# Norm weight and inverse rms split in the FFN of a two-block transformer kernel, and rope totals first in the latent expansion

## The reference, cut to what matters

```python
def _rmsnorm(x, g):
    xf = x.astype(jnp.float32)
    y = xf * lax.rsqrt(jnp.mean(xf * xf, axis=-1, keepdims=True) + EPS)      # EPS = 1e-6
    return (y * g.astype(jnp.float32)).astype(x.dtype)

# first block, its last two steps (D_MODEL = 1024, D_FF = 2816)
x = x + _rmsnorm(_memory_cross_attention(h, mem, ...), norm_mem_post)
h = _rmsnorm(x, norm_ffn_pre)
g, u = jnp.split(h @ w_gate_up, 2, axis=-1)
x = x + _rmsnorm((jax.nn.silu(g) * u) @ w_down, norm_ffn_post)

# second block, latent attention: 4 heads, nope 128 wide, rope 64 wide
q = (_rmsnorm_2(c_q, q_a_norm_w) @ w_uq).reshape(b, s, 4, 192)
kv = (_rmsnorm_2(c_kv, kv_a_norm_w) @ w_ukv).reshape(b, s, 4, 256)
k_nope, v_mla = kv[..., :128], kv[..., 128:]
q_m = _rmsnorm_2(jnp.concatenate([q_nope, q_rope], axis=-1), mla_q_norm_w)
k_m = _rmsnorm_2(jnp.concatenate([k_nope, k_rope], axis=-1), mla_k_norm_w)
o_mla = _mla_attention(q_m, k_m, v_mla)
```

## Time and profile before

| what | value |
|---|---|
| median of 3 runs | 3254.81 us (3250.01 to 3255.03) |
| the profiled execution | 3254.06 us |
| its span, first to last instruction | 3252.3 us |
| mean granted TensorE clock | 0.978 of full |
| TensorE (PE) busy | 3082.2 us, 95% of the span |
| VectorE (DVE) busy | 1711.2 us, 53% |
| GpSimd (POOL) busy | 1373.1 us, 42% |
| ScalarE (ACT) busy | 1053.8 us, 32% |

### The profile page before, as it was taken

How to read it: one execution, slowest core, us unless ns; L and a number is a source line. 1 busy time by engine, 2 the same in 40 slices (tenths; PEclk the granted TensorE clock), 3 DMA queues, 4 the chain that set the end, 5 groups by cost and what they waited for, 6 DMA issues and landing times.

```text
span 3252.3 us, 37435 instructions
## 1 busy us (share of the span) xinstructions
PE 3082.2 (95%) x13379; PEld 2409.0 (74%) x13390; DVE 1711.2 (53%) x2554; ACT 1053.8 (32%) x1638; POOL 1373.1 (42%) x799
## 2 busy tenths in 40 slices
PE   8999998999988899999999799879999989999998
PEld 6788785668776588888888576648766778878886
DVE  3799965545443621121212731135796576666648
ACT  3321215620334300000010333135676366662221
POOL 3254332334432233343434143256000367777878
PEclk9899999999999999999999899999999999999999
DMA  3022410024210011111111113351441247779774
GB/s 106 27 91 90 146 48 14 1 98 187 66 51 20 26 46 52 46 50 47 47 50 46 41 53 120 98 168 52 114 117 65 98 164 272 261 276 394 260 248 171
DMA packets 118695, 351.96 MB, mean 108 GB/s; under 512 B 12844, under 2 KB 24276, under 8 KB 117816
## 3 DMA queue, kind: packets, MB, share of 16 engines
q1 hardware_dynamic: 88064, 275.55, 25.0%
q10 hardware_dynamic: 30520, 74.93, 6.2%
HBM read 246.61 MB, written 103.57 MB: 108 GB/s over the span
## 4 chain that ended last, share of the span: by engine, by line
PE 80%; DVE 9%; ACT 4%; issue 3%; POOL 2%; DMA 2%; SPq 0%; ACTq 0%; POOLq 0%; DVEq 0%
PE ps L829 23%; PE ps L831 22%; PE ps L830 22%; PE ps L875 3%; PE ps L1047 2%; PE ps L1383 1%; PE ps L1371 1%; POOL left_lo L708 1%; PE ps L1037 1%; PE ps L1356 1%; POOL part_in L703 1%; DMA x_kept_scratch<-x 1%; DVE x L2260 1%; DVE y L2259 1%; PE ps L1357 1%
## 5 line engine op out<-in xcount | busy, mean ns | idle before, releaser
L566 POOL TENSOR_TENSOR w_hi<-w_raw,zero 128x1024 fp32r<-128x1024 f32 x133 | 252.9, 1901 | 950.1 <-PE ps L831 943.4
L829 PE MATMUL ps<-normed_hi,w_hi 128*128 128x512 f32 x976 | 384.9, 394 | 8.7 <-DVEq L2473 4.2
L831 PE MATMUL ps<-normed_hi,w_lo 128*128 128x512 f32 x976 | 380.4, 390 | 0.0
L830 PE MATMUL ps<-normed_lo,w_hi 128*128 128x512 f32 x976 | 380.2, 390 | 0.0
L708 POOL TENSOR_TENSOR left_lo<-part_in,left_hi 128x512 fp32r<-128x512 f32 x208 | 286.8, 1390 | 139.0 <-ACT left_hi L2052 93.4
L569 POOL TENSOR_TENSOR w_lo<-w_raw,w_hi 128x1024 fp32r<-128x1024 f32 x133 | 338.1, 2542 | 10.4
L829 PEld LDWEIGHTS ps<-normed_hi,w_hi 128*128 128x128 f32 x976 | 183.6, 188 | 50.6 <-issue 12.4
L2482 DVE TENSOR_TENSOR tmp<-tmp,ps 128x1024 f32<-128x1024 f32 x22 | 26.9, 1222 | 368.4 <-PE ps L831 367.9
L830 PEld LDWEIGHTS ps<-normed_lo,w_hi 128*128 128x128 f32 x976 | 183.7, 188 | 39.8 <-issue 2.2
L831 PEld LDWEIGHTS ps<-normed_hi,w_lo 128*128 128x128 f32 x976 | 183.5, 188 | 38.4
L829 PE MATMUL ps<-h_hi,w_hi 128*128 128x512 f32 x528 | 207.2, 393 | 1.4 <-ACT wi_t L1597 1.4
(11 more groups left out here) (478 smaller groups left out, 7492.7 us busy)
## 6 DMA issues: line engine op xcount, KB each, us to landing
w_raw<-weights_dram SPq DMA_DIRECT2D x164, 512.0 KB, 3.3
part_in<-mlp_weights_dram SPq DMA_DIRECT2D x144, 256.0 KB, 4.7
mlp_parts_scratch<-part_t SPq DMA_DIRECT2D x64, 512.0 KB, 4.5
down_t<-mlp_parts_scratch SPq DMA_DIRECT2D x64, 512.0 KB, 7.0
mlp_parts_scratch<-part_b SPq DMA_DIRECT2D x32, 512.0 KB, 5.0
down_b<-mlp_parts_scratch SPq DMA_DIRECT2D x32, 512.0 KB, 5.9
gates_scratch<-tmp ACTq DMA_DIRECT2D x24, 512.0 KB, 2.6
gated<-gates_scratch ACTq DMA_DIRECT2D x24, 512.0 KB, 5.2
```

Source lines behind the costliest of these rows:

```text
L566: nc.gpsimd.tensor_tensor(w_hi[s][:], raw[s][:], zero[:, 0:1].broadcast_to([P, 1024]), ALU.add).then_inc(w_rounded, 1)
L829: nc.tensor.matmul(out, sh, mh, start=start, stop=False)
L830: nc.tensor.matmul(out, sh, ml, start=False, stop=False)
L831: return nc.tensor.matmul(out, sl, mh, start=False, stop=stop)
```

## The change

Three edits come together.

In the FFN, h = x * weight * r, with r the inverse rms of a token, is split. VectorE and ScalarE now make x * weight alone, each tile as soon as its residual is made: ScalarE rounds x times the weight to the high part, VectorE makes the low part from x, weight and high part in one operation. r is applied later: VectorE multiplies the gate product by r before Silu. The up product keeps the factor 1/r, which stays in hidden, in y and in its mean square; the post norm divides it out again. For that its guard EPS is multiplied by the mean square (with EPS) of x, which is kept in `ffn_mean` and added once to the sum of squares. TensorE's totals of x go in between the first tiles, in slot 3 instead of 2, and the products that keep it busy are 40 instead of 22. The zeroing of `y` stands behind the increment of `f_added`.

In the latent expansion the rope part of each total comes first, ahead of the wait for the square, and it waits for `g_rs` in its place. The four stores of v move from ScalarE's queue to SP's, behind the weight loads.

```diff
@@ SP
             load_slabs(2, SLABS["out_2"][0] + 2)
+            sp.wait_ge(v_act, 4)
+            sp.wait_ge(v_dve, 4)
+            for hd in range(MLA_HEADS):
+                sp.dma_start(t["mla_v"][hd], v_value[:, :, hd * P:(hd + 1) * P]).then_inc(v_stored, 16)
             sp.wait_ge(v_stored, 16 * MLA_HEADS)
@@ TensorE
-            def first_tiles(slabs, name, src):
+            def first_tiles(slabs, name, src, busy=22, totals=False):
                 tiles, before = PRE[name]
-                kept_busy(22)
+                kept_busy(busy)
                 for s in range(2):
                     pe.wait_ge(w_split, SLABS[slabs][0] + s + 1)
                 for k in range(tiles):
+                    if totals and k:
+                        total_tile(name, k - 1, 3)
+                    if totals and k == tiles - 1:
+                        total_tile(name, k, 3)
                     pe.wait_ge(n_lo, before + k + 1)
@@
             total_added(1)
-            total("ffn_pre")
@@ ffn_chunk
                     pe.wait_ge(w_split, 12 * c + s0 + 2 * j + 2)
+                    if first == j:
+                        pe.wait_ge(n_rs, 5)
                     tile(1, 0, normed, KT, 2 * (j % 2) + 1).then_inc(w_used, 1)
@@
-            first_tiles("ffn", "ffn_pre", normed)
+            first_tiles("ffn", "ffn_pre", normed, 40, True)
@@ head_total
-                pe.wait_ge(g_sq, e + 1)
                 if e == 0:
                     pe.wait_ge(rope_sq, 3)
+                elif e >= 2:
+                    pe.wait_ge(g_rs, e - 1)
                 hd, is_q = e // 2, e % 2
-                over_features(wide(2 + e % 2), tmp[e % 2], ones[:], True, False)
                 rope = q_rope_sq[:, hd // 2, :] if is_q else k_rope_sq[:]
-                over_features(wide(2 + e % 2), rope, halves[:, 1 + (hd % 2 if is_q else 0), :],
-                              False, True).then_inc(g_tot, 1)
+                over_features(wide(2 + e % 2), rope, halves[:, 1 + (hd % 2 if is_q else 0), :], True, False)
+                pe.wait_ge(g_sq, e + 1)
+                over_features(wide(2 + e % 2), tmp[e % 2], ones[:], False, True).then_inc(g_tot, 1)
@@ ScalarE
             inverse(3)
-            squares("ffn_pre", lambda k: x[:, k, :], lambda k: (x_added, KT + k + 1))
-            inverse(4)
-            round_hi("ffn_pre", normed[0])
+            for k in range(KT):
+                act.wait_ge(x_added, KT + k + 1)
+                nc.scalar.activation(normed[0][:, k, :], x[:, k, :], ACT.Copy, scale=col("ffn_pre", k)).then_inc(n_hi, 1)
+                square_tile("ffn_pre", k, x[:, k, :], (x_added, KT + k + 1))
+            act.wait_ge(n_sum, 5)
+            step(nc.scalar.activation(ffn_mean[:], wide(3), ACT.Ln, bias=eps[:], scale=1.0 / D))
+            nc.scalar.activation(acc[:], ffn_mean[:], ACT.Exp, scale=-0.5).then_inc(n_rs, 1)
+            step(nc.scalar.activation(ffn_mean[:], ffn_mean[:], ACT.Exp))
@@ ffn_hidden
-                    act.wait_ge(w_used, 12 * c + s0 + 2 * j + 1)
-                    act.wait_ge(f_lo, 4 * c + j + 1)
-                    nc.scalar.activation(tmp[j % 2][:], wide(2 * (j % 2)), ACT.Silu).then_inc(f_silu, 1)
+                    act.wait_ge(f_scaled, 4 * c + f_scaled_0 + j + 1)
+                    nc.scalar.activation(tmp[j % 2][:], tmp[j % 2][:], ACT.Silu).then_inc(f_silu, 1)
@@
-            inverse(5)
+            inverse(5, guard=zero)
@@
-            act.wait_ge(v_act, 4)
-            act.wait_ge(v_dve, 4)
-            for hd in range(MLA_HEADS):
-                act.dma_start(t["mla_v"][hd], v_value[:, :, hd * P:(hd + 1) * P]).then_inc(v_stored, 16)
@@ VectorE, add_square
+                if post == 2 and k == 1:
+                    step(stt(acc[:], ffn_mean[:], EPS * D / P, acc[:], ALU.mult, ALU.add))
@@
-            residual(3, "mem_post")
-            scaled(4, "ffn_pre", x, normed)
+            before = PRE["ffn_pre"][1]
+
+            def ffn_rest(k):
+                dve.wait_ge(n_hi, before + k + 1)
+                stt(normed[1][:, k, :], x[:, k, :], col("ffn_pre", k), normed[0][:, k, :].bitcast(F32), ALU.mult,
+                    ALU.subtract).then_inc(n_lo, 1)
+
+            dve.wait_ge(n_rs, 4)
+            for k in range(KT):
+                step(stt(y[:, k, :], y[:, k, :], col("mem_post", k), acc[:], ALU.mult, ALU.mult))
+                tt(x[:, k, :], x[:, k, :], y[:, k, :], ALU.add).then_inc(x_added, 1)
+                if k:
+                    ffn_rest(k - 1)
+            ffn_rest(KT - 1)
+            dve.sem_inc(n_tmp, KT)
 
             dve.sem_inc(f_lo, 2)
+            dve.sem_inc(f_added, 8)
             nc.vector.memset(y[:], 0.0).then_inc(y_zero, 1)
             dve.wait_ge(y_zero, 1)
-            dve.sem_inc(f_added, 8)
             s0 = SLABS["ffn"][0]
+            dve.wait_ge(n_rs, 5)
@@ ffn_hidden
                     part = tmp[j % 2]
+                    dve.wait_ge(w_used, 12 * c + s0 + 2 * j + 1)
+                    dve.wait_ge(f_lo, 4 * c + j + 1)
+                    tt(part[:], wide(2 * (j % 2)), acc[:], ALU.mult).then_inc(f_scaled, 1)
                     dve.wait_ge(w_used, 12 * c + s0 + 2 * j + 2)
```

More of the change, by code:

```diff
@@ L241, in program @@
         halves = at("halves", AR + 60 * KB, [P, 3, P])
+        ffn_mean = at("ffn_mean", late_at, [P, S])
         cos, sin = at("cos", late_at, [P, S]), at("sin", late_at + 4 * KB, [P, S])
@@ L408, in program @@
         stored = sem("stored")
+        f_scaled, f_scaled_0 = m_qk, 2 * MEM_HEADS
         pair_landed, late_landed, landed_0 = gates_in, staged, 16 * 12
@@ L881, in total_added, with total_tile @@
                 over_features(wide(2), acc, ones[:]).then_inc(n_sum, 1)
-            def total_tile(name, k):
+            def total_tile(name, k, slot=2):
                 tiles, before = PRE[name]
                 pe.wait_ge(n_sq, before + k + 1)
-                over_features(wide(2), tmp[k % 2], ones[:], k == 0, k == tiles - 1).then_inc(
+                over_features(wide(slot), tmp[k % 2], ones[:], k == 0, k == tiles - 1).then_inc(
                     n_sum if k == tiles - 1 else n_added, 1)
@@ L1557, in post_square, with inverse @@
                 nc.scalar.activation(tmp[k % 2][:] if k else acc[:], src, ACT.Square).then_inc(n_post_sq, 1)
-            def inverse(r, width=D, dst=None):
+            def inverse(r, width=D, dst=None, guard=eps):
                 act.wait_ge(n_sum, r + 1)
-                step(nc.scalar.activation(acc[:], wide(2), ACT.Ln, bias=eps[:], scale=1.0 / width))
+                step(nc.scalar.activation(acc[:], wide(2), ACT.Ln, bias=guard[:], scale=1.0 / width))
                 nc.scalar.activation(acc[:] if dst is None else dst, acc[:], ACT.Exp, scale=-0.5).then_inc(n_rs, 1)
```

## The result

| | before | changed |
|---|---|---|
| median (range) | 3253.19 us, 4 runs (3250.01 to 3255.03) | 3225.72 us, 4 runs (3222.49 to 3227.26) |
| profiled execution, span | 3254.06, 3252.3 us | 3227.26, 3225.5 us |
| mean granted clock | 0.978 | 0.980 |

The ratio is 0.9915, 95% interval 0.9898 to 0.9932: 27.5 us less, where 26.0 were forecast.

A forecast was written before the change was run, and what follows sets the result against it. TensorE, busy 95% of the span, was taken as the bound, so time returns only where it waits or runs at its lower clock. 13.0 - 1.0 + 14.0 = 26.0 us less than 3254.81 gives 3229 us, range 3221 to 3239.

The forecast's parts named there:

- FFN entry: FFN entry: next gate tile starts at 1106.0 instead of 1119.0, TensorE pacing at 4.46 us a tile; gain 13.0 us.
- Rival C: FFN entry: busy products at half speed throughout, entry gain 5 instead of 13 us, 3237 us in all; chance 0.06.
- E's condition: Whole kernel: more gain if the clock never falls and loads aren't slowed, 3224 us; chance 0.08.
- Loop: FFN loop: the new gate multiplication and Silu, 2.3 us, end 8 us before the up product; cost nothing.
- rival D: FFN loop: the new multiplication sits on TensorE's path and costs 50 us, slower at 3279 us; chance 0.03.
- Tail: FFN tail: one scaled addition of 1.28 us between the sums of squares loses about 1.0 us, bounds 0 to 2.3.
- Expansion: Latent expansion: earlier first total, shorter rounds and earlier head 0 loads gain 14 us, bounds 9 and 17.
- Rival A: Latent expansion: head 0's loads and split give less, gain 8 instead of 14 us, 3235 us in all; chance 0.15.
- Head 0 is late next: Behind the expansion: head 0's loads and split limit the gain; GpSimd about 10 us earlier, first maximum 13.1 us earlier.
- The rule against it: FFN entry and latent expansion: frequent tiny idles between short matmul groups would make the clock swing again; no size given.
- Rival B: Expansion or FFN entry: the clock falls, 1.7 us each, three falls 5 us, 3234 us in all; chance 0.12.

The follow-up runs named there:

- kernel 12: The changed kernel run again with the same code, beside the guard and v-split runs; 3226.72 us, ratio 0.9919 to the kernel before.
- kernel 1: The kernel before with the FFN edits alone, the latent expansion as before; 3238.99 us, ratio 0.9962 to the kernel before.
- 6: The changed kernel with the zeroing of y ahead of its increment of 8 again; 3223.27 us, ratio 0.9909 to the kernel before.
- kernel 7: The changed kernel with rope totals first only in rounds 0 to 2, old order from round 3; 3223.06 us, ratio 0.9914 to the kernel before.
- kernel 8: The changed kernel with six more gate multiplications per FFN tile, same result written again; 3226.29 us, ratio 0.9925 to the kernel before.
- kernel 10: The changed kernel with head 0's logits no longer waiting for its last v split; 3221.83 us, ratio 0.9903 to the kernel before.
- 11: The changed kernel with both the guard one addition earlier and the later wait for head 0's v split; 3223.54 us, ratio 0.9911 to the kernel before.
- 5: The changed kernel with 22 busy products instead of 40 ahead of the FFN's first tile; 3223.18 us, ratio 0.9911 to the kernel before.
- Kernel 9: The changed kernel with the guard's addition one addition earlier, behind y's second addition; 3220.67 us, ratio 0.9901 to the kernel before.
- kernel 4: The kernel before with only the rope totals first, v's stores still on ScalarE; 3245.37 us, ratio 0.9981 to the kernel before.
- 3: The kernel before with only v's four stores moved from ScalarE to SP; 3243.51 us, ratio 0.9976 to the kernel before.
- kernel 2: The kernel before with the two expansion edits alone, the FFN as before; 3237.12 us, ratio 0.9958 to the kernel before.

## Why the prediction was right

The mechanism held in each stage; that the sum of 26.0 came so near owes something to luck. In the first trace the four forecast terms give 14.5 + 1.5 - 0.55 + 15.6 = 31.1 us, and two stretches that the prediction put at nothing take back 1.0 and 3.4. Of the 5 us over the forecast, 4.3 lie in the two executions that were compared: 1.1 and 1.5 us of clock in the FFN, 1.7 in the expansion. With kernel 12's trace for the changed kernel, and kernel 1's expansion for the one of before, the terms are 13.4, 0.0, -0.5 and 13.8, 26.7 in all. In the times, 3225.72 is 3.1 us under the forecast; 1.6 of it is that the median of before came out as 3253.19 instead of 3254.81.

**FFN entry: forecast 13.0.** The stretch shows 14.5 in the first trace and 13.4 when the same kernel was run again (67.60), 13.3 in kernel 1. The steps hold: first low part 1068.4 (forecast 1068.7), 8.93 us for the busy products (9.2), 4.49 us a tile (4.46), last product of these tiles done at 1104.6 (1106.0), TensorE paces. The one assumed figure was 1.2 us for the clock (without it the prediction's own numbers give a gain of 14.1, not the 14.3 of its bounds), and the runs show two outcomes for it. Inverse to tail is one of two values: 730.6 to 730.8 in six traces (changed, 6, 7, 8, 10, 11), 733.1 to 733.8 in the other four with the FFN edits (1, 5, 9, 12). In the changed kernel's trace, of the first kind, the clock never falls; windows of kernel 12, the same code, show the second kind:

```profile
1058.00:1066.00 8.00, 8.00 (x56) 7.38 (x55) 4.42 (x4) 4.08 (x4) 0.00 (x0) 0.79 0.19 66
...
1784.00:1788.00 4.00, 2.89 (x7) 2.31 (x8) 1.05 (x1) 0.00 (x0) 0.00 (x0) 0.62 0.41 131
```

Its second row is the other half of the difference. TensorE waits 2.8 us for the last hidden tile, before and after the change alike; in before and in kernel 12 the clock then falls (0.60 and 0.62), in the changed kernel's trace not. Before, then changed:

```profile
1800.00:1804.00 4.00, 4.00 (x13) 3.14 (x11) 1.25 (x2) 0.82 (x1) 0.00 (x0) 0.60 0.26 107
```

```profile
1784.00:1788.00 4.00, 3.28 (x14) 2.70 (x15) 2.07 (x3) 0.32 (x1) 0.00 (x0) 1.00 0.41 131
```

That is the 1.5 us that the table gives to the loop, and nothing of the change's: kernel 4, which has none of the FFN edits, keeps the clock at 1.00 there too and takes 664.01 us to the tail, as the changed kernel does (664.12). Rival C (busy products at half speed throughout) didn't happen in any of the ten traces, E's condition for the entry did in six.

**Loop: forecast nothing.** Right; kernel 8 kills rival D with 7.3 us a tile to spare.

**Tail: forecast -1.0.** It is -0.55, within the bounds of 0 to 2.3, and in the traces of kernels 1 and 5 it is -0.1 and -0.2 (23.91 and 23.99). Kernel 9 shows it all to be placement.

**Expansion: forecast 14.0.** First total 9.1 us earlier behind v (33.79 to 24.66; forecast 8.9; 8.2 counted from kernel 1). A pair of rounds takes 43.16 / 3.5 = 12.3 us (forecast 11.9). The store of round 1 comes 11.9 earlier (11.3). Here is the step that was off: loads were to take 0 to 3 us longer because two more stores fall among them. They took 16.59 us from that store to GpSimd's start, 17.43 before and 16.75 in kernel 1, so not longer; GpSimd starts 12.8 us earlier (11.2 counted from kernel 1) instead of 10. The split then took 25.1 us instead of 24.4, and from its end to the first maximum it was 4.9 instead of 3.9 (TensorE at a granted clock of 0.50 for all of the first logits, behind the wait of 11.55), so the first maximum came 14.2 us earlier, 12.5 counted from kernel 1, forecast 13.1. Rival A is out. "Head 0 is late next" is right, and kernels 7 and 10 bracket it: 9.1 us taken from the rounds behind it cost 2.6, and 5.3 us taken from its split bring 2.8, each time until the last store decides.

**The rule against it.** Before, the clock from first product to last total was 0.92; with the change it is 1.00 for 48 us. The Trainium skill, page "TensorE: Matmul & The Clock Gate", section "A second HAM failure mode: psum-queue depth-cycling", has frequent small idles make the clock swing. The trace of before agrees in one round of seven; the changed kernel's doesn't, with TensorE busy 46.27 of 48.20 us. Rival B's falls stayed away from the expansion. That the shorter idles did this is not shown. In the old order, with waits of 1.1 to 2.1 us ahead of the totals, the clock from first to last logarithm of the rounds was 0.97 before and 0.93 in kernel 7 (falls in one and in two rounds), but 1.00 in kernels 1 and 3. In the new order it was 1.00 in all ten traces.

**The sum.** By the times of kernels 1 and 2 the FFN gives 11.8 and the expansion 13.7 us. Kernel 1's trace has the first of these in the stretches of the FFN and behind it: entry 13.3, loop 0.0, tail -0.1, and -1.3 between post norm and v (last section). At the third maximum the expansion's gain is 15.6 us by the trace of before (forecast 14); by kernel 1's, which has that code too, it is 13.9, and kernel 2's time has 13.7 (interval 9 to 18 us).

## What to carry to other kernels

A norm's inverse can be applied behind the product, if an engine is idle there: here one multiplication per tile, hidden with over 7 us to spare, took a chain of eight scalings off the path. Before moving an engine's DMA issues, look for the queue that has nothing due: four issues of 4.6 to 4.8 us together are covered on SP, while on ScalarE they cost 7.3 us of run time. When a stage gets faster, name what is late next and count only up to it: of 18.6 us taken between first product and last total, 15.6 arrived at the third maximum. And compare a stage with more than one trace of the same code: 1.7 of those 15.6 us belonged to the one trace of before.

## What the runs showed that was not expected

**The same code at two clocks.** The entry and the last tile of the FFN meet the lower clock in some executions and not in others, 2.3 to 3.2 us in all, with the same instructions; kernels 6, 10 and the first trace of the change are at 730.6, kernel 12 at 733.2. Behind the wait of 2.8 us at the last tile the granted clock was 0.57 to 0.64 in seven of the fourteen traces and 1.00 in the other seven. What decides between the two was not found. It is about as large as kernel 10's gain and several times the guard's cost, so a small edit has to be read from the stretch it touches, not from the time.

**A loss 200 us behind the edit.** From post norm to v, nothing was changed, yet every kernel with the FFN edits takes 247.9 to 248.3 us there except 9 and 11 (246.7), and those without take 246.8 to 247.0. Windows around the same stretch of the gates, before and changed:

```profile
2034.00:2045.00 11.00, 11.00 (x48) 9.01 (x47) 0.26 (x1) 0.00 (x0) 0.22 (x1) 0.94 0.24 96
```

```profile
2018.40:2029.40 11.00, 11.00 (x43) 8.95 (x42) 0.28 (x1) 0.00 (x0) 0.00 (x0) 0.84 0.24 97
```

TensorE is busy throughout in both, at 0.94 and 0.84, with 48 and 43 products done. That is about 1.1 us (0.10 of 11, or five products of 0.228), the size of the loss. The other twelve traces bear it out in the same 11 us: 0.81 to 0.84 with 42 or 43 products in every kernel that has the loss, 0.91 to 0.96 with 46 to 48 in those that haven't, 9 and 11 (0.96, 48) among them. So the loss is clock and not work. Why placing the guard one addition earlier, over 200 us ahead, keeps it away is not known.
